# Writing a sparse gate matrix by indirect scatter transfers instead of one-hot matmuls, in a one-core PEER layer on Trainium2

## The chip, the cores and the metric

The kernel runs on one core of one Trainium2 chip. The time is the device time of one launch, in microseconds (us). Before the change it is 4085.16 us, the median of three runs (4085.02 to 4093.54).

## What is computed

One inference step of a one-layer encoder for 544 tokens (512 of a prompt, 32 of a sample), width 2048, in float32. First a convolution group and a gated linear attention group are mixed and normalised. Then comes the PEER mixer, in which the change lies:

```python
q = (xt @ w_query).reshape(tp, PEER_HEADS, 2, PEER_DKEY // 2)
s = jnp.einsum('thpc,hpnc->thpn', q, sub_keys)
sv, si = lax.top_k(s, PEER_TOPK)                       # 8 heads, 2 x 128 keys, top 16
cand = sv[:, :, 0, :, None] + sv[:, :, 1, None, :]
cid = si[:, :, 0, :, None] * PEER_NKEYS + si[:, :, 1, None, :]
best, pos = lax.top_k(cand.reshape(...), PEER_TOPK)    # 16 of 256 pairs
ids = jnp.take_along_axis(cid..., pos, axis=-1)        # expert numbers, 0 to 16383
gates = jax.nn.softmax(best, axis=-1)
h = gelu(einsum('td,thkd->thk', xb, u_table[ids]))
out = einsum('thk,thkd->td', gates * h, v_table[ids])
```

So each token has 128 pairs (expert, gate); an expert can be picked by more than one head of a token, and its gates then add.

## The kernel before, in words

Engines are programmed by hand and joined by semaphores. Activations lie feature-major (128 features on the partitions, tokens along the row). A product in float32 is made of three products of split halves: each 128x2048 weight tile is loaded by SyncE (SP) into one of two buffers `wraw`, ScalarE (ACT) copies it to the reduced-precision `wh` (line 837), and another engine subtracts, `wl = wraw - wh`; TensorE (PE) then runs `xh*wh`, `xl*wh` and `xh*wl` over 16 feature tiles and two halves of the tokens, 96 matmuls of 128x272 a tile (`job`, line 522). GpSimd (POOL) makes all splits `wl` up to the last tile of U (`lo`, line 460, semaphore `wlo`); VectorE (DVE) makes those of V (`v_lo_split`, line 1502, semaphore `v_lo`). SP loads the next tile of a buffer when the split of its last one is done.

The stages, in time: input products, convolution and attention (to about 780 us of the profiled execution); `w_out` (16 tiles) with the first normalisation; `w_q` (16 tiles) with the key scores; **the U stage**, 128 tiles of the expert table U, which gives h for all 16384 experts and all tokens; **the V stage**, 128 tiles of V, which multiplies W = gate * h with V.

Of the 544 tokens 416 are handled densely (`TD`): for them the gates stand in a full matrix G of 16384 experts x 416 tokens, which lies in DRAM (`g_dram`) like h (`h_dram`). The other 128 tokens take their rows of V and their h one by one with indirect gathers by POOL in the V stage (`h_gather` and `v_gather`, lines 486 to 496; 128 of each, 128 elements of 4 bytes or 128 rows of 8 KB in one).

How G is made before: DVE does the top-k of the eight heads (lines 1411 to 1430), ACT and DVE the softmax (line 1077, lines 1433 to 1440); DVE makes the indices of the sparse tokens (lines 1445 to 1451). After 16 tiles of U (`U_A` = 4 loops of four) PE waits for the picks, turns them with 12 transposes (line 761) and waits for ACT's copy of them (line 1080). In the next 52 tiles of U (`U_B` = 13 loops of four) two `g_group`s follow each tile: for four tokens each, DVE writes one-hot rows (`oneA` in three bf16 parts that hold the gate, line 1468, and `oneB`, line 1469), PE multiplies them (12 matmuls of 128x128, line 745) into a 128x128 slice of G of that token, ACT copies the slices to `gst` (line 1087) and stores 2 MB per 32 tokens in DRAM (line 1098). The last 60 tiles of U (`U_C`) have no such work.

In the V stage the experts are taken in 16 groups of eight tiles. SP loads the group's G (`gt`) and h (`hg`), 1664 KB each (`group_in`, line 413), in the same queue as the tiles of V. The first group's load waits until all of G is stored. DVE makes `wt = hg * gt` and its split for the next group (`make_w`, line 1482), adds PE's results (line 1500), adds the sparse tokens' rows (line 1519) and splits V (line 1506). At the turn from U to V, DVE, ACT and DVE again make the first W in a chain (lines 1532, 1111, 1527), and POOL splits the second tile of V beside it.

Of the kernel before, what the change touches and what calls it, by code (L numbers as in the profile page):

```python
# [30 lines left out]
P = 128  # L31
# [15 lines left out]
TT = 5  # L47
# [11 lines left out]
G_AHEAD = 2  # L59
# [62 lines left out]
def program(nc, xT, w_in, w_f, w_out, w_q, u_t, v_t, conv_state, conv_w, conv_vec, gla_state,  # L122
# [3 lines left out]
    with ctx:  # L126
# [5 lines left out]
        def sem(name):  # L132
# [89 lines left out]
        picksT = at("picksT", [P, 3, TD], F32, S0 + 7840)  # L222
        gate_p = [at(f"gate_p{a}", [P, TD], F32, S0 + 12832 + a * ROWD) for a in range(3)]

        assert 12832 + 3 * ROWD == 17824
# [8 lines left out]
        OH = 2 * 4 * P * 2  # L234
        gst = [at("gst0", [P, P, GC], F32, M0 + 4 * ROW), at("gst1", [P, P, GC], F32, M1 + 4 * OH)]
        part = at("part", [P, TD], BF16, M1 + 4 * OH + P * GC * 4)
        oneA = [at(f"oneA{a}", [P, 2, 4, P], BF16, M1 + a * OH) for a in range(3)]
        oneB = at("oneB", [P, 2, 4, P], BF16, M1 + 3 * OH)

# [8 lines left out]
        gt = at("gt", [P, NGC, EG, GC], F32, S0)  # L248
# [44 lines left out]
        q_out, s_mm, s_out, topk_s, gd_s, ge_s, picks_s, pt_mm, pt_out = (  # L293
            sem("q_out"), sem("key_scores"), sem("key_scores_out"), sem("head_picked"), sem("gate_diff"),
            sem("gate_exp"), sem("picks_ready"), sem("picks_turned"), sem("picks_turned_out"))
        oneh, g_mm, g_out = sem("one_hots"), sem("g_mm"), sem("g_out")
        g_st, h_st = [sem("g_stored0"), sem("g_stored1")], [sem("h_stored0"), sem("h_stored1")]
# [8 lines left out]
        ids_s, rows_in, v_lo, slot_s, y_sp_s, y_turn = (  # L306
            sem("slot_ids"), sem("v_rows_laid"), sem("v_lo_split"), sem("slot_added"),
            sem("slots_done"), sem("slots_turned"))
        sh_in = [sem(f"slot_h_in{b}") for b in range(SLOTS // HB)]
        sv_in = [sem(f"slot_v_in{b}") for b in range(3)]  # L310

# [5 lines left out]
        h_dense = h_flat[NKEY * P * SD:].rearrange("(n p u t) -> n p u t", p=P, u=2, t=TD)  # L317
# [7 lines left out]
        U_A, U_B = 4, NGC  # L325
        U_C = NKEY // 4 - U_A - U_B
# [33 lines left out]
        def _(sp):  # L360
# [41 lines left out]
            with sp.Fori(0, NG) as g:  # L402
                for m in range(EG):
                    sp.wait_ge(wlo, g * EG + (A_U + m - 1))
                    tile(us[bass.ds(g, 1), m].rearrange("o p k c -> (o p) k c"), m % 2)
                    for d in range(2):
                        load(v_dst[bass.ds(g, 1), m, d].rearrange("o j e c -> (o j) e c"),
                             v_src[bass.ds(g, 1), m, d].rearrange("o j e c -> (o j) e c"), rows_in)
            gsrc = g_dram.rearrange("c j (g e) t -> g j c (e t)", e=EG)
            hsrc = h_dense.rearrange("(g n) p u t -> g p n (u t)", n=EG // 2)  # L410
            vs = v_t.rearrange("(g n u) p k c -> g n u p k c", u=2, n=EG // 2)

            def group_in(g):
                for dst, src, q in ((gt[:].rearrange("p c e t -> p c (e t)"), gsrc, g_in),
                                    (hg[:].rearrange("p (n u) t -> p n (u t)", u=2), hsrc, h_in)):
                    a = src[g] if isinstance(g, int) else src[bass.ds(g, 1)].rearrange("o p n q -> (o p) n q")
                    load(dst, a, q)

            def v_first():
                for m in range(4):  # L420
                    sp.wait_ge(wlo, A_V + m - 1)
                    tile(vs[0, m // 2, m % 2], m % 2)

            def v_pairs(g, i0, i1):
                with sp.Fori(i0, i1) as i:
                    for u in range(2):
                        sp.wait_ge(v_lo, (g * EG + (u - 3)) + i * 2)
# [9 lines left out]
            v_first()  # L437
# [19 lines left out]
        def _(pool):  # L457
# [26 lines left out]
            lo_pairs(A_Q // 2 + 1, A_V // 2 + 1)  # L484
# [34 lines left out]
        def _(pe):  # L519
            mat = nc.tensor.matmul  # L520

            def job(u, n, ah, al, out, waits, first_k=None, ks=range(KT), begin=True, end=True):


                if begin:
                    pe.wait_ge(wlo, n + 1)
# [13 lines left out]
            pe.sem_inc(g_mm, G_AHEAD)  # L540
# [193 lines left out]
            def u_tile(n, u):  # L734

                job(u, n + A_U, xh, xl, zr(u), [(h_out, n + 1)])

            def g_group(q, v, bank):

                pe.wait_ge(oneh, q + 1)  # L740
                pe.wait_ge(g_out, q + 1)
                for t in range(4):
                    o_ps = ps[:, bank, t * P:(t + 1) * P]
                    for a in range(3):
                        ins = mat(o_ps, oneB[:, v, t], oneA[a][:, v, t], start=(a == 0), stop=(a == 2))  # L745
                ins.then_inc(g_mm, 1)

            pe.wait_ge(q_out, NQ)
            with pe.Fori(0, U_A) as i:
                for w in range(4):  # L750
                    u_tile(i * 4 + w, w % 2)


            pe.wait_ge(picks_s, 1)
            pe.wait_ge(s_out, NQ)
            for a in range(3):
                for tt, (t0, m) in enumerate(TOPK_TILES):
                    if tt == SPARSE:
                        continue
# [902 lines left out]
```

## Time and profile before

| what | us |
|---|---|
| median of three runs | 4085.16 |
| lowest, highest | 4085.02, 4093.54 |
| the profiled execution, its own time | 4094.46 |
| its span in the profile | 4092.7 |

The profile is of one execution with a hardware profiler. Its page gives the busy time of each engine, the span in 40 slices of 102.3 us, the chain of work that ended last, and the costliest groups of instructions. "L534" is line 534 of the kernel. PE is TensorE, PEld its weight loads, DVE VectorE, ACT ScalarE, POOL GpSimd, SP the queue of SyncE; a name with a q (SPq, ACTq) is an engine's sequencer, which issues transfers. "Idle before" is the time in which an engine stood still just ahead of an instruction, with what ended it.

### The profile page before, as it was taken

To read this page: it belongs to the slowest core of one execution; us is meant where nothing else is said; L and a number is where in the kernel's file an instruction comes from. 1 tells how busy PE (TensorE), PEld (TensorE's weight loads), DVE (VectorE), ACT (ScalarE), POOL (GpSimd) and SP (SyncE) were. 2 spreads that over 40 slices of the span, in tenths; PEclk is the share of its full clock that TensorE was granted. 3 is DMA by queue.
4 is the path that set the end of the run, shared out by engine and by line. 5 is a ranking of instruction groups with operands and counts; after the bars stand their busy time and mean duration, and the time that the engine had idled before them with its cause. 6 is when DMAs were issued, how large, how long until landed. Compare 5 with 4: busy or idle time off the path is not lost.

```text
span 4092.7 us, 70828 instructions
## 1 busy us (share of the span) xinstructions
PE 3908.7 (96%) x27864; PEld 3831.7 (94%) x27864; DVE 2617.1 (64%) x4474; ACT 1051.8 (26%) x914; POOL 1470.2 (36%) x497
## 2 busy tenths in 40 slices
PE   8999998796999999999999999999999999999996
PEld 7999998796999999999999999999999999999995
DVE  5776957656899299999972000001587787887867
ACT  3222322323222233333332222222222221222213
POOL 3232332344333333333334333434444344442311
PEclk9988988898999999999999999999999999999998
DMA  3221221221235656666666666665677778778752
GB/s 136 79 72 59 81 65 72 80 82 52 82 123 166 199 192 211 218 224 210 225 213 200 198 194 199 198 199 192 234 266 293 294 287 313 265 286 311 279 208 85
DMA packets 416196, 751.55 MB, mean 184 GB/s; under 512 B 19600, under 2 KB 343632, under 8 KB 355296
## 3 DMA queue, kind: packets, MB, share of 16 engines
q1 hardware_dynamic: 351936, 543.27, 39.4%
q0 software_dynamic: 22528, 134.30, 8.2%
q10 hardware_dynamic: 41632, 72.67, 5.0%
q8 instruction: 61, 1.00, 0.1%
q14 instruction: 39, 0.32, 0.0%
HBM read 677.60 MB, written 206.78 MB: 216 GB/s over the span
## 4 chain that ended last, share of the span: by engine, by line
PE 76%; DVE 14%; DMA 4%; issue 2%; ACT 2%; POOL 1%; SPq 1%; ACTq 0%; DVEq 0%; POOLq 0%
PE ps L534 52%; PE ps L778 19%; DMA wraw<-in_v_t 4%; DVE yb L1305 2%; PE ps L745 2%; DVE wl L1506 2%; PE ps L656 1%; PE ps L611 1%; PE ps L658 1%; ACT wh L837 1%; SPq L362 1%; DVE acc L1500 1%; DVE y_sp L1519 1%; DVE yfb L1314 0%; POOL wl L464 0%
## 5 line engine op out<-in xcount | busy, mean ns | idle before, releaser
L464 POOL TENSOR_TENSOR wl<-wraw,wh 128x2048 fp32r<-128x2048 f32 x202 | 961.0, 4758 | 1753.3 <-ACT wh L837 1753.3
L534 PE MATMUL ps<-xh,wh 128*128 128x272 f32 x5888 | 1241.3, 292 | 50.8 <-POOL xl L483 22.0
L534 PE MATMUL ps<-xh,wl 128*128 128x272 f32 x5888 | 1228.6, 290 | 0.0
L534 PE MATMUL ps<-xl,wh 128*128 128x272 f32 x5888 | 1225.2, 290 | 0.0
L534 PEld LDWEIGHTS ps<-xh,wh 128*128 128x128 f32 x5888 | 935.2, 191 | 63.9 <-issue 52.7
L534 PEld LDWEIGHTS ps<-xl,wh 128*128 128x128 f32 x5888 | 936.1, 191 | 0.0
L534 PEld LDWEIGHTS ps<-xh,wl 128*128 128x128 f32 x5888 | 930.5, 191 | 0.0
L837 ACT ACTIVATE wh<-wraw 128x2048 fp32r<-128x2048 f32 x328 | 628.5, 1916 | 1145.5 <-PE ps L778 732.8
L778 PE MATMUL ps<-Wh,wh 128*128 128x416 f32 x2048 | 721.9, 352 | 29.3 <-DVE wl L1506 21.2
L778 PE MATMUL ps<-Wh,wl 128*128 128x416 f32 x2048 | 724.8, 354 | 0.0
L778 PE MATMUL ps<-Wl,wh 128*128 128x416 f32 x2048 | 717.4, 350 | 0.0
L1468 DVE TENSOR_SCALAR oneA<-iota,picksT,gate_p 128x128 bf16<-128x128 f32 x1248 | 577.5, 516 | 62.5 <-PE ps L745 62.1
L489 POOL DMA_INDIRECT gath<-v_rows,s_ids x128 | 301.9, 2359 | 594.2 <-DVE y_sp L1519 556.4
L1532 DVE TENSOR_TENSOR wt<-hg,gt 128x416 f32<-128x416 f32 x8 | 4.6, 591 | 670.2 <-PE ps L534 670.0
L778 PEld LDWEIGHTS ps<-Wh,wh 128*128 128x128 f32 x2048 | 386.3, 189 | 36.6 <-issue 34.3
L778 PEld LDWEIGHTS ps<-Wl,wh 128*128 128x128 f32 x2048 | 386.7, 189 | 6.3
L778 PEld LDWEIGHTS ps<-Wh,wl 128*128 128x128 f32 x2048 | 385.9, 188 | 2.6
L1055 ACT ACTIVATE hb<-ps 128x544 f32<-128x544 f32 x128 | 79.9, 624 | 1144.5 <-PE ps L534 1144.5
L1506 DVE TENSOR_TENSOR wl<-wraw,wh 128x2048 fp32r<-128x2048 f32 x126 | 288.1, 2286 | 62.5 <-ACT wh L837 62.3
L1519 DVE SCALAR_TENSOR_TENSOR y_sp<-gath,s_w,y_sp 128x2048 f32<-128x2048 f32 x127 | 298.7, 2352 | 5.7
L1500 DVE TENSOR_TENSOR acc<-acc,ps 128x416 f32<-128x416 f32 x256 | 150.0, 586 | 183.7 <-PE ps L778 179.2
L1305 DVE SCALAR_TENSOR_TENSOR yb<-ext,cwt,yb 128x574 f32<-128x574 f32 x232 | 212.7, 978 | 1.7
(235 smaller groups left out, 2906.4 us busy)
## 6 DMA issues: line engine op xcount, KB each, us to landing
wraw<-in_u_t SPq DMA_DIRECT2D x128, 1024.0 KB, 5.0
v_rows<-in_v_t SPq DMA_DIRECT2D x256, 512.0 KB, 6.9
wraw<-in_v_t SPq DMA_DIRECT2D x128, 1024.0 KB, 5.1
wraw<-in_w_in SPq DMA_DIRECT2D x40, 1024.0 KB, 5.0
h_scratch<-hb ACTq DMA_DIRECT2D x64, 416.0 KB, 3.9
g_scratch<-gst ACTq DMA_DIRECT2D x13, 2048.0 KB, 7.7
gt<-g_scratch SPq DMA_DIRECT2D x16, 1664.0 KB, 14.1
hg<-h_scratch SPq DMA_DIRECT2D x16, 1664.0 KB, 20.5
```

Source lines behind the costliest of these rows:

```text
L464: nc.gpsimd.tensor_tensor(wl[:, u], wraw[:, u], f(wh[:, u]), ALU.subtract).then_inc(wlo, 1)
L489: nc.gpsimd.indirect_dma_start(gath[s % 3][:], None, v_rows, bass.IndirectOffsetOnAxis(ap=s_ids[:, s:s + 1], axis=0)).then_inc(sv_in[s % 3 ...
L534: ins = mat(out[:, h], w[:, u, k], m[:, k, halves[h]], start=(begin and k == ks[0] and w is wh and m is ah), stop=(end and k == ks[-1] and ...
L745: ins = mat(o_ps, oneB[:, v, t], oneA[a][:, v, t], start=(a == 0), stop=(a == 2))
L778: ins = mat(yd(u, d), w[:, u, d * EG + e], m[:, e], start=(e == 0 and w is wh and m is Wh[v]), stop=(e == EG - 1 and w is wl))
L837: go(wh[:, u], wraw[:, u], ACT.Copy).then_inc(whi, 1)
L1055: C.done(go(parts(hb[:, w // 2, w % 2]), zr(w % 2), ACT.Gelu), h_out)
L1305: ins = stt_(y_[:], rows, tap, y_[:], ALU.mult, ALU.add)
L1468: ts_(oneA[a][:, u, t], iota[:], picksT[:, 1, tok], gate_p[a][:, tok], ALU.is_equal, ALU.mult)
L1500: C.done(tt_(a_, a_, yd(n % 2, d), ALU.add), y_add)
L1506: C.inc(tt_(wl[:, n % 2], wraw[:, n % 2], f(wh[:, n % 2]), ALU.subtract), v_lo)
L1519: C.inc(stt_(y_sp[:], gath[s % 3][:], s_w[:, s:s + 1], y_sp[:], ALU.mult, ALU.add), slot_s)
```

## The change

G in DRAM is laid out anew, as (group, row of 128, expert tile in the group, token), and is cleared: ACT stores a block of zeros (128 x 4 x 416, 832 KB) 32 times during the `w_out` stage, two stores after each tile. DVE sets the block once ahead of that stage, and waits for the 32 stores before it writes the first `x2t`, since the block lies in that place. After the softmax DVE computes the element number of each pick in G, and POOL issues 512 indirect transfers (8 heads x 16 ranks x 4 tiles of tokens), each of which adds up to 128 elements of 4 bytes from SBUF to G in DRAM (`compute_op=add`); a token is one partition, so the elements of one transfer differ. Between two heads POOL waits until all transfers of the heads before have landed. SP waits for the last before it loads the first group.

The transposes, one-hots, G matmuls, G copies and 2 MB stores are gone. POOL splits tiles up to the 16th of U only; DVE splits from there on (`lo` on DVE, semaphore `dlo`, `D0` = 16 tiles after the start of U), the first two of V included, and computes `acc` between the first 16 of these splits. The h scratch is laid out so that a partition's part of a group is one run; the loads of `gt` and `hg` each read one run of 13,312 bytes per partition where they read 13 runs of 1 KB and 4 runs of 3,328 bytes.

```diff
+        g_col = [at(f"g_col{i}", [P, TT, P], dt, S0 + 7840 + i * TT * P * 4) for i, dt in enumerate((F32, F32, U32))]
+        g_idx = g_col.pop()
+        zeros = at("zeros", [P, 4, TD], F32, S0)
...
-        gt = at("gt", [P, NGC, EG, GC], F32, S0)
+        gt = at("gt", [P, EG, TD], F32, S0)
...
+        g_rows = g_flat.rearrange("(g j e t) -> g j e t", j=P, e=EG, t=TD)
...
+        h_dense = h_flat[NKEY * P * SD:].rearrange("(g p n u t) -> g n p u t", g=NG, p=P, u=2, t=TD)
...
+        D0 = A_U + 4 * U_A
...
@@ block.sync, loads of U @@
+            with sp.Fori(3, NG) as g:
+                for m in range(EG):
+                    sp.wait_ge(dlo, g * EG + (A_U + m - 1 - D0))
+                    u_tile_in(g, m)
...
-            for v in range(2):
-                sp.wait_ge(g_st[v], 16 * (NGC // 2 + 1))
+            sp.wait_ge(g_put, 16 * len(G_TILES) * SLOTS)
             for v in range(2):
                 sp.wait_ge(h_st[v], 32 * (EG // 4))
             group_in(0)
-            v_first()
+            v_pairs(0, 0, EG // 4)
...
@@ block.gpsimd @@
-            lo_pairs(A_Q // 2 + 1, A_V // 2 + 1)
+            lo_pairs(A_Q // 2 + 1, D0 // 2)
...
+            pool.wait_ge(g_ids, 1)
+            pool.wait_ge(g_zero, 16 * 2 * NG)
+            for h in range(PH):
+                if h:
+                    pool.wait_ge(g_put, 16 * len(G_TILES) * TOPK * h)
+                for k in range(TOPK):
+                    for tt in G_TILES:
+                        m, c = TOPK_TILES[tt][1], h * TOPK + k
+                        nc.gpsimd.indirect_dma_start(
+                            g_elem, bass.IndirectOffsetOnAxis(ap=g_idx[0:m, tt, c:c + 1], axis=0),
+                            picks[0:m, 0, tt, h, k:k + 1], None, compute_op=ALU.add).then_inc(g_put, 16)
...
@@ block.tensor, U stage @@
-            pe.wait_ge(picks_s, 1)
...
-                    ins = nc.tensor.transpose(ps[:, 4 + a, t0:t0 + m], src, ident[0:m, 0:m])
-            ins.then_inc(pt_mm, 1)
-            pe.wait_ge(pt_out, 1)
-            with pe.Fori(0, U_B) as i:
+            with pe.Fori(U_A, NKEY // 4) as i:
                 for w in range(4):
-                    u_tile(i * 4 + (4 * U_A + w), w % 2)
-                    for q in range(2):
-                        g_group(i * 8 + (2 * w + q), q, 4 + (2 * w + q) % 4)
...
+                    n = i * 4 + w
+                    job(w % 2, n + A_U, xh, xl, zr(w % 2), [(h_out, n + 1)], split=(dlo, n + (A_U + 1 - D0)))
...
@@ block.scalar, w_out stage @@
                     go(sq[:], r1[:, bass.ds(n, 1)].rearrange("p o t -> p (o t)"), ACT.Square).then_inc(rsq_s, 1)
+                    a.wait_ge(zero_set, 1)
+                    g = g_rows[bass.ds(n, 1)].rearrange("o j e t -> (o j) e t")
+                    for e in (0, 4):
+                        a.dma_start(g[:, e:e + 4], zeros[:]).then_inc(g_zero, 16)
...
@@ block.vector @@
+            nc.vector.memset(zeros[:], 0.0).then_inc(zero_set, 1)
             nc.vector.memset(sum1[:], 0.0)
...
             norm_stats(D, sum1, sum2, tmp[0], yr)
+            v_.wait_ge(g_zero, 16 * 2 * NG)
...
-            v_.wait_ge(pt_out, 1)
...
+            C.done(cp(g_idx[:], flat(1)), dve)
+            C.done(ts_(g_idx[:], g_idx[:], EG - 1, None, ALU.bitwise_and), dve)
+            C.done(cp(g_col[0][:], g_idx[:]), dve)
+            C.done(ts_(g_col[0][:], g_col[0][:], float(TD - P * TD), None, ALU.mult), dve)
+            C.done(stt_(g_col[1][:], flat(1), float(P * TD), g_col[0][:], ALU.mult, ALU.add), dve)
+            C.done(stt_(g_col[0][:], flat(2), float(EG * TD), g_col[1][:], ALU.mult, ALU.add), dve)
+            for tt in G_TILES:
+                ins = ts_(g_col[1][:, tt], g_col[0][:, tt], s_tok[:], float(TOPK_TILES[tt][0]), ALU.add, ALU.add)
+            C.done(ins, dve)
+            for tt in G_TILES:
+                ins = cp(g_idx[:, tt], g_col[1][:, tt])
+            C.done(ins, g_ids)
+
+            def lo(n, u):
+                v_.wait_ge(whi, n + 1)
+                v_.wait_ge(mm, n - 1)
+                C.inc(tt_(wl[:, u], wraw[:, u], f(wh[:, u]), ALU.subtract), dlo)
+
+            with C.loop(KT // 2, {dlo: 2, dve: 4}) as i:
                 for u in range(2):
-                    v_.wait_ge(g_mm, i * 2 + (u + 1))
...
+                    lo(i * 2 + (D0 + u), u)
+                    kk = bass.ds(i * 2 + u, 1)
+                    C.done(ts_(one(acc[:, kk]), one(f(xh[:, kk])), ALPHA, None, ALU.mult), dve)
+                    C.done(stt_(one(acc[:, kk]), one(f(xl[:, kk])), ALPHA, one(acc[:, kk]), ALU.mult, ALU.add), dve)
+            with C.loop((A_V + 2 - D0 - KT) // 2, {dlo: 2}) as i:
+                for u in range(2):
+                    lo(i * 2 + (D0 + KT + u), u)
             v_.sem_inc(acc_set, 1)
```

## Rows read from the trace of the kernel before

**Rows 1.** The page: the DMA engines' busy tenths in 40 slices

```profile
DMA  3221221221235656666666666665677778778752
```

**Rows 2.** The page: the chain that ended last, shares by engine

```profile
PE 76%; DVE 14%; DMA 4%; issue 2%; ACT 2%; POOL 1%; SPq 1%; ACTq 0%; DVEq 0%; POOLq 0%
```

**Rows 3.** The chain in time: start, us, engine, tile, line, count; U stage to V

```profile
1249.02 170.60 PE ps L534 x1344
1423.64 13.81 PE ps L534 x96
...
2123.91 721.66 PE ps L534 x5760
...
2853.42 156.30 PE ps L778 x816
```

**Rows 4.** Groups of instructions over the whole span

```profile
L464 POOL TENSOR_TENSOR wl<-wraw,wh 128x2048 fp32r<-128x2048 f32 x202 | 961.0, 4758 | 1753.3 <-ACT wh L837 1753.3
...
L1506 DVE TENSOR_TENSOR wl<-wraw,wh 128x2048 fp32r<-128x2048 f32 x126 | 288.1, 2286 | 62.5 <-ACT wh L837 62.3
...
L745 PE MATMUL ps<-oneA,oneB 128*128 128x128 bf16 x1248 | 78.7, 219 | 0.0
```

**Rows 5.** What PE waited for: first 1225 to 2850, then 2840 to 4060 us

```profile
PE ps L534 <- ACT picksT L1080: 2.2, 1, 2.2
...
PE ps L778 <- DVE wl L1506: 21.2, 13, 5.7
PE ps L778 <- DVE Wl L1527: 7.9, 1, 7.9
```

**Rows 6.** Timeline of ACT before the 17th tile of U (start, us)

```profile
1384.21 1.92 ACT L837 ACTIVATE wh<-wraw 128x2048 fp32r<-128x2048 f32 x1
...
1396.24 1.92 ACT L837 ACTIVATE wh<-wraw 128x2048 fp32r<-128x2048 f32 x1
```

**Rows 7.** Timeline of DVE, softmax and the indices of the sparse tokens

```profile
1376.35 0.82 DVE L1438 TENSOR_REDUCE gsum<-picks 128x40 f32<-128x640 f32 x1 [32.48 <-ACT picks L1077]
...
1377.64 1.92 DVE L1440 TENSOR_TENSOR picks<-picks,gsum 128x640 f32<-128x640 f32 x1
...
1381.16 0.23 DVE L1451 CAST s_hid<-s_h 128x128 uint32<-128x128 f32 x1
```

**Rows 8.** Timeline of POOL, the first 32 gathers of h, back to back

```profile
2852.99 1.28 POOL L494 DMA_INDIRECT s_h<-h_scratch,s_hid  x1 [0.16 <-issue]
...
2866.92 2.88 POOL L494 DMA_INDIRECT s_h<-h_scratch,s_hid  x1 [0.31 <-issue]
...
2901.32 0.94 POOL L489 DMA_INDIRECT gath<-v_rows,s_ids  x1 [0.30 <-issue]
```

**Rows 9.** Timeline of DVE beside the second row above

```profile
2866.68 2.29 DVE L1506 TENSOR_TENSOR wl<-wraw,wh 128x2048 fp32r<-128x2048 f32 x1 [1.29 <-ACT wh L837]
```

**Rows 10.** The gathers of V rows (ns, min/median/max), and landing of the h gathers

```profile
L489 POOL DMA_INDIRECT gath<-v_rows,s_ids x128: 937/2748/3008, 2901.3 to 3940.3; - x128
...
DMA to landing us min/median/max: 4.4/6.7/10.9
```

**Rows 11.** Windows: w_out, then U alone (PE, PEld, DVE, ACT, POOL busy, PEclk, DMA, GB/s)

```profile
780.00:950.00 170.00, 170.00 (x1336) 170.00 (x1337) 97.38 (x57) 32.68 (x27) 66.72 (x14) 0.98 0.25 86
...
2200.00:2400.00 200.00, 200.00 (x1599) 200.00 (x1598) 0.00 (x0) 40.65 (x32) 77.03 (x17) 1.00 0.61 196
```

**Rows 12.** DMA issues on SP: KB each, median us to landing

```profile
gt<-g_scratch SPq DMA_DIRECT2D x16, 1664.0 KB, 14.1
hg<-h_scratch SPq DMA_DIRECT2D x16, 1664.0 KB, 20.5
```

**Rows 13.** Timeline of SP: first group's load, and one in the V stage

```profile
2807.39 2.46 SPq L362 DMA_DIRECT2D gt<-g_scratch  x1
...
3679.06 9.79 SPq L362 DMA_DIRECT2D hg<-h_scratch  x1
```

**Rows 14.** Timeline of DVE, the first write of x2t

```profile
970.05 1.36 DVE L1385 TENSOR_TENSOR x2t<-r,sum 128x544 f32<-128x544 f32 x2 [0.79 <-ACT sum L854]
```

More of the change, by code:

```diff
@@ L401, in _, with u_tile_in @@
             v_dst = v_rows.rearrange("(g e j) (i d c) -> g i d j e c", e=EG, j=P, i=EG, d=2)
-            with sp.Fori(0, NG) as g:
+            def u_tile_in(g, m):
+                a = us[g, m] if isinstance(g, int) else us[bass.ds(g, 1), m].rearrange("o p k c -> (o p) k c")
+                tile(a, m % 2)
+                for d in range(2):
+                    to = v_dst[g, m, d] if isinstance(g, int) else v_dst[bass.ds(g, 1), m, d].rearrange("o j e c -> (o j) e c")
+                    fr = v_src[g, m, d] if isinstance(g, int) else v_src[bass.ds(g, 1), m, d].rearrange("o j e c -> (o j) e c")
+                    load(to, fr, rows_in)
@@ L403, in _ @@
+            with sp.Fori(0, 2) as g:
                 for m in range(EG):
                     sp.wait_ge(wlo, g * EG + (A_U + m - 1))
[L405 to L409, printed above, removed]
@@ L410, in _ @@
-            hsrc = h_dense.rearrange("(g n) p u t -> g p n (u t)", n=EG // 2)
+                    u_tile_in(g, m)
+            assert D0 == A_U + 2 * EG
+            for m in range(EG):
+                if m < 2:
+                    sp.wait_ge(wlo, D0 + m - 1)
+                else:
+                    sp.wait_ge(dlo, m - 1)
+                u_tile_in(2, m)
+            with sp.Fori(3, NG) as g:
+                for m in range(EG):
+                    sp.wait_ge(dlo, g * EG + (A_U + m - 1 - D0))
+                    u_tile_in(g, m)
@@ L411, in _ @@
+            gsrc = g_rows.rearrange("g j e t -> g j (e t)")
             vs = v_t.rearrange("(g n u) p k c -> g n u p k c", u=2, n=EG // 2)
             def group_in(g):
[L414 to L422, printed above, removed]
+                for dst, src, q in ((gt, gsrc, g_in), (hg, h_group, h_in)):
+                    a = src[g] if isinstance(g, int) else src[bass.ds(g, 1)].rearrange("o p q -> (o p) q")
+                    load(dst[:].rearrange("p e t -> p (e t)"), a, q)
             def v_pairs(g, i0, i1):
@@ L520, in _, with job @@
             mat = nc.tensor.matmul
-            def job(u, n, ah, al, out, waits, first_k=None, ks=range(KT), begin=True, end=True):
+            def job(u, n, ah, al, out, waits, first_k=None, ks=range(KT), begin=True, end=True, split=None):
                 if begin:
-                    pe.wait_ge(wlo, n + 1)
+                    s, v = split or (wlo, n + 1)
+                    pe.wait_ge(s, v)
                     for s, v in waits:
@@ L1101, in _ @@
[L1101 to L1107 removed]
+            u_four(1, 1)
+            with C.loop(NG - 2, {h_out: EG}) as g:
+                for i in range(2):
+                    u_four(g + 2, i)
             for e in range(EG):
@@ L1137, in _ @@
             a.wait_ge(cst_out, 32)
-            for v in range(2):
-                a.wait_ge(g_st[v], 16 * (NGC // 2 + 1))
+            a.wait_ge(g_zero, 16 * 2 * NG)
             for v in range(2):
@@ L1473, in _, with flat @@
-            v_.wait_ge(g_mm, TD // 4 + G_AHEAD)
-            for v in range(2):
-                v_.wait_ge(g_st[v], 16 * (NGC // 2 + 1))
-            with C.loop(KT, {dve: 2}) as k:
-                kk = bass.ds(k, 1)
-                C.done(ts_(one(acc[:, kk]), one(f(xh[:, kk])), ALPHA, None, ALU.mult), dve)
-                C.done(stt_(one(acc[:, kk]), one(f(xl[:, kk])), ALPHA, one(acc[:, kk]), ALU.mult, ALU.add), dve)
+            def flat(a):
+                return picks[:, a].rearrange("p t h k -> p t (h k)")
```

140 lines of the change are left out of this document (36 added, 104 removed).

## The prediction, made before the changed kernel ran

> **What bounds the kernel now.** I read the page's chain first: 76% of it is PE [rows 2]. Then the same chain in order of time. In the U stage it is PE tile after tile; from the 17th tile, which starts at 1423.64 us, to 2123.91 us lie the 52 tiles with G work, then 60 tiles without take 721.66 us, and at 2853.42 us V starts [rows 3]. PE's waits in the U stage are one: 2.2 us for ACT's copy of the turned picks [rows 5]. So between 1249 and 2845 us the time is the length of PE's own list, and whatever leaves that list leaves the time, as long as no other engine or transfer comes later than PE. In the V stage PE waits 21.2 us for DVE's V splits in 13 places and 7.9 us once for the first W [rows 5]; the DMA engines are busier there (tenths of 7 and 8) than in the U stage (6) [rows 1].
>
> **The change, part by part.**
>
> 1. *G work leaves PE.* With it a tile takes (2123.91 - 1423.64)/52 = 13.47 us, without it 721.66/60 = 12.03 us [rows 3]. Gain 52 x 1.44 = 74.8 us. (The 1248 matmuls are listed with 78.7 us busy [rows 4], the same size.)
>
> 2. *Transposes and the wait for their copy.* The 16th tile ends at 1249.02 + 170.60 = 1419.62, the 17th starts at 1423.64 [rows 3]: gain 4.0 us. DVE's one-hots and ACT's copies were beside PE and give nothing.
>
> 3. *Does DVE split in time?* The 17th tile's `wh` is copied at 1396.24 to 1398.16 [rows 6]; the DVE split takes 2.29 us where POOL's takes 4.76 [rows 4], so `wl` can stand at 1400.5, 19 us before PE wants it at 1419.6. Ahead of it on DVE stands the new index work. It begins after 1381.16 + 0.23 = 1381.4 [rows 7]: six instructions over 640 columns and eight over 128. A pass over 640 columns took 0.82 us and one took 1.92 [rows 7]; with 0.3 for each small one the whole is 7.3 to 13.9 us, done at 1388.7 to 1395.3, before the split. Cost nothing; its cover is 19 us. Later each tile gives DVE 2.3 us (4.3 with `acc`) in 12.03. The next load of a buffer is issued when the split is done, so it starts 2.5 us earlier than now. No gain from that, as PE never waited for `wl` here [rows 5].
>
> 4. *POOL's 512 scatters.* POOL's last split, of tile 16, starts when ACT ends at 1386.13 [rows 6] and takes 4.76: POOL is free at 1390.9. Take 1391 as the first scatter, 1395 at the latest. No scatter stands in the trace. Nearest are the gathers of h, also 128 elements of 4 bytes: the first 32, back to back, took from 2852.99 to 2901.32 [rows 8], 1.51 us apart. A quiet one takes 0.94, and one took 2.88, having started in the 0.24 us behind a DVE split of 2.29 us, which it outlasts [rows 8, 9]; in the U stage DVE splits once in 12.03 us, less often than there, so 1.51 is a fair pitch. The far end is the V-row gather, median 2.75 [rows 10] and 0.3 of issue: 3.05. I take 1.51, because size and count of the elements agree: 512 x 1.51 = 773 us, and seven waits between heads of 6.7 us each, the landing of an h gather [rows 10], 47 us. G is complete at 1391 + 820 = 2211 us. It is wanted when SP comes to the first group's load: that is at 2807.39 now [rows 13], 38 us before the U stage ends at 2845.57; after the change U ends at 1419.62 + 112 x 12.03 = 2767, so at 2729. Slack 518 us; cost nothing. The cover is gone at a pitch of (2729 - 1391 - 47)/512 = 2.52 us.
>
>    The Trainium skill ("SBUF — State Buffer", section "Summary: rules for kernel authors") says that GpSimd and a DVE instruction with two SBUF inputs block one another fully when GpSimd reads SBUF too, and that descriptor generation starves under DVE's faster modes. The 2.88 us row agrees with blocking. If every scatter met a whole split, the pitch would be near the V-row gather's, which is the far end above.
>
> 5. *What the DMA engines carry.* The U stage alone has them at 0.61 [rows 11]. 416 tokens x 128 picks over 16 engines are 3328 elements each. In the 1338 us from 1391 to 2729 the free share is 0.39 x 1338 = 522 us, or 0.157 us per element. The h gathers fed 8 elements per engine every 1.51 us (0.19 each) into a V stage of 7 tenths [rows 1] that hardly stopped PE [rows 5]; the price of an element that is read, added and written in DRAM isn't shown. Below it may be hidden, above 0.157 it may stretch the U stage; I take hidden, the nearest row being the gather.
>
> 6. *The clearing.* 32 stores of 832 KB in a stage that moves 86 GB/s at a share of 0.25 [rows 11]; two per tile of about 12 us add 142 GB/s, 228 in all, no more than the V stage moves. ACT is busy 32.68 of 170 us there [rows 11] and takes two issues in. The last pair is issued near 955; if it takes 14.1 us, as the twice as large load of `gt` [rows 12], it lands at 969, and DVE wants it at 970.05 [rows 14]. Cost 0, bounds 0 and 10 (it may share the engines with the first loads of `w_q` and the keys). The memset runs beside PE's first tile.
>
> 7. *The turn to V.* PE waits 7.9 us now [rows 5], since DVE's first split of W is held up by POOL's split of the second V tile. In its place DVE makes that split first: Gelu and ACT's copy of 1.92 us [rows 6], DVE's split 2.29 [rows 4], then product, copy and split of one 128x416 slice; with an estimated 0.6 us for each of the four short ones it is 6.6 us, with handovers 7. Gain 1, bounds -3 and 4.
>
> 8. *The V stage.* `gt` and `hg` come in long runs. Their loads take 14.1 and 20.5 us to land [rows 12], and one issue held SP for 9.79 us [rows 13], with the V tiles' loads behind it in the queue. If shorter runs were the reason, both shrink, and the waits for V splits go with them: 21.2 us is the most, 0 the least. I take 12.
>
> Sum: 74.8 + 4.0 + 1 + 12 = 91.8 us. The profiled execution took 4094.46 us, which becomes 4002.7. It stands 9.3 us over the median of the runs, 4085.16, so for the median 4085.2 - 91.8 = 3993 us. Without the 12 us it is 4005, with all 21.2 it is 3984.
>
> **Rivals.**
>
> *A. The issue of scatters is slow (slower than before).* Place: SP's wait for the last scatter. Each scatter costs 3.05 us, as the V-row gathers. Then G is complete at 1391 + 512 x 3.05 + 47 = 3000 us. The first group wants 38 us more to V's start, as now: 3038 against 2774 in my forecast, so 264 us late, 3993 + 264 = 4257 us. It turns to slower from a pitch of 2.52 + 91.8/512 = 2.70 us. For it: the accumulate form may need more per element than a gather, and those V-row gathers stood beside DVE's work. Against: the V-row gathers come singly, right as a DVE split starts; back to back the same form took 0.94 [rows 8].
>
> *B. The elements are taken one after another (slower by far).* An h gather's 8 elements per engine land in 6.7 us [rows 10], 0.84 us each. Gathers overlap, 4 of them in flight at a pitch of 1.51. If an add in DRAM does not overlap, because a read must come back before its write, then 3328 x 0.84 = 2787 us, G is complete at 4178, and the end is near 3993 + (4178 + 38 - 2774) = 5435 us. In milder form, 0.5 us per element, 1664 us, it is 3993 + 319 = 4312 us. The Trainium skill ("DMA: Bandwidth & Descriptors", section "Rules for kernel authors") says that the accumulate reads its destination and writes it later, with nothing held in between. Its section "Anatomy of one DMA — SWDGE (gpsimd) path" gives about 2.0 us fixed for one transfer; 512 of them one behind another would be an estimated 1024 us and still be hidden.
>
> *C. Issue hidden, loads late.* The elements cost 0.2 us of the DMA engines each: 666 us against 522 free, the U stage is stretched by up to 144 us for tiles that wait for their load: 3993 + 144 = 4137 us at the worst; a half of that, 4065, is still faster. Against: a buffer's load is issued some 5 us after a tile ends (copy 1.92 us [rows 6], split 2.29 [rows 4] and Gelu) and is wanted 24.06 us after it, so it may take 19 us.
>
> *D. The V loads do not get shorter and the clearing is late:* 4005 + 10 = 4015 us, still faster. It is a part of the forecast's own range, 3980 to 4020.
>
> **How the numbers follow.** Forecast with D: 0.64. C: 0.06, half on either side of before. A, and pitches between 2.52 and 3.05: 0.14, of which 0.02 end below the time before. B: 0.16. A measurement of this kernel can tell about 0.2%, 8 us, from no change. Faster: 0.64 + 0.02 + 0.02 = 0.68; same 0.02; slower 0.30. The range must leave out no more than 0.2: from 3980 over D, C and A to 4260 it leaves out B and little else. The likeliest case's own range is 3980 to 4020.
>
> **What the profile of the changed kernel would show.** Right: tiles of U 12.03 us apart from 1249 us to about 2767; no wait of PE for `wl` there; 512 DMA_INDIRECT on POOL from 1391 us, about 1.5 apart in runs of 64, ending near 2211; DMA share in that time under 0.9; V starting at about 2774; PE's waits in V under 21 us. Wrong: SP idle until POOL's last scatter lands, with PE waiting in front of V (A, B; a POOL that is busy means A, a POOL that waits between heads or stands in long issues means B); tiles of U further apart with PE waiting for ACT's and DVE's splits (C); DVE's first `x2t` later than 970 (D).

## The result, and the profile after

The changed kernel takes 3978.55 us in the median of four runs (3974.40 to 3983.18), the kernel before 4089.32 in its four; the ratio is 0.9729, 95% interval 0.9715 to 0.9743. The forecast was 3993 us with a range from 3980 to 4260. The direction and the likeliest case were right, and the time lies 1.5 us under the range. The profiled execution took 3983.18 us, 111.3 less than the one before.

From the page of the kernel after, its span, two engines and the DMA slices:

```profile
span 3981.4 us, 64674 instructions
...
PE 3814.9 (96%) x26604; PEld 3745.5 (94%) x26604; DVE 2230.6 (56%) x2933; ACT 939.1 (24%) x809; POOL 1821.2 (46%) x895
...
DMA  3211222353225677777777777665578778777752
```

The chain that ended last in the kernel after, in order of time (start, us):

```profile
770.58 171.01 PE ps L554 x1344
...
1239.28 1517.51 PE ps L554 x12096
...
2763.74 809.71 PE ps L767 x4272
```

The U stage, broken up by the G work in [rows 3], is now one unbroken run of PE from its third tile on, 126 tiles from 1239.28 to 2756.79 us. That makes 12.04 us a tile.

Where the 111.3 us of the two profiled executions lie, with the starts of `w_out`'s run of tiles and the ends of U as the marks:

| stretch | before | after | gain |
|---|---|---|---|
| start to `w_out` | 779.96 | 770.58 | 9.4 |
| `w_out` to the end of U | 2065.6 | 1986.2 | 79.4 |
| end of U to the first V matmul | 7.9 | 7.0 | 0.9 |
| V and the rest | 1239.3 | 1217.7 | 21.6 |

The first row is a stretch that the change does not touch. The last is larger than the 12 us of the forecast.

The scatters, DVE's U splits and PE's V matmuls in the list of groups of the kernel after:

```profile
L513 POOL DMA_INDIRECT g_scratch<-picks,g_col x512 | 869.9, 1699 | 199.5 <-issue 179.5 <-DMA g_scratch<-picks,g_col 19.9
...
L1437 DVE TENSOR_TENSOR wl<-wraw,wh 128x2048 fp32r<-128x2048 f32 x114 | 261.5, 2294 | 1099.8 <-ACT wh L824 1005.6
```

All seven waits between heads together are 19.9 us. What PE waited for from 2760 to 3960 us, which answers to [rows 5]:

```profile
PE ps L767 <- DVE Wl L1494: 7.0, 1, 7.0
PE ps L767 <- DVE wl L1473: 4.5, 3, 2.5
```

POOL's timeline of the first scatters and of the last, and below it DVE's split and index work beside them:

```profile
1393.21 1.72 POOL L513 DMA_INDIRECT g_scratch<-picks,g_col  x1 [0.17 <-issue]
...
1398.97 1.35 POOL L513 DMA_INDIRECT g_scratch<-picks,g_col  x1 [0.30 <-issue]
1400.62 3.59 POOL L513 DMA_INDIRECT g_scratch<-picks,g_col  x1 [0.30 <-issue]
1404.52 1.55 POOL L513 DMA_INDIRECT g_scratch<-picks,g_col  x1 [0.30 <-issue]
...
2459.97 2.47 POOL L513 DMA_INDIRECT g_scratch<-picks,g_col  x1 [0.30 <-issue]
```

```profile
1371.52 0.49 DVE L1421 CAST g_col<-picks 128x640 uint32<-128x640 f32 x1
...
1376.27 5.04 DVE L1431 CAST g_col<-g_col 128x128 uint32<-128x128 f32 x4
1400.50 2.29 DVE L1437 TENSOR_TENSOR wl<-wraw,wh 128x2048 fp32r<-128x2048 f32 x1 [19.19 <-ACT wh L824]
```

From 1393.21 to 2459.97 lie 511 steps: 2.09 us each with the waits between heads, 2.05 without them, where the forecast had 1.51 without them. A quiet scatter takes 1.55 us (1.35 with the 32-token tile) and 0.30 of issue. The one that starts at 1400.62 runs into DVE's split of 1400.50 to 1402.79 and takes 3.59, which is 2.04 more. The split had 2.17 us left when that scatter started. The Trainium skill ("SBUF — State Buffer", section "Summary: rules for kernel authors") has a GpSimd operation that reads SBUF and a DVE instruction with two SBUF inputs block each other fully; these rows agree. Besides, POOL stops for 1.7 to 5.7 us after every 72nd scatter, seven times and 26 us more than the usual 0.30 in all; the profile puts these stops to issue, and what they are is not shown. The four small casts at the end of the index work took 5.04 us together, beside POOL's own split (1376.48 to 1381.08); the index work ended at 1381.3, well before DVE's first U split at 1400.50.

The clearing cost nothing. The first `x2t` is written 189.9 us after the start of `w_out`'s run (190.1 before, [rows 14]); the stores land in 5.0 us each:

```profile
960.44 1.36 DVE L1349 TENSOR_TENSOR x2t<-r,sum 128x544 f32<-128x544 f32 x2 [0.78 <-ACT sum L839]
```

```profile
g_scratch<-zeros ACTq DMA_DIRECT2D x32, 832.0 KB, 5.0
```

### The profile page after: what moved, and what is told of

Read it like the earlier page. It is cut to its first block, busy times and chain, and to the rows that moved or that the text cites. A ratio compares the mean times of both kernels' runs of the same rounds, so it can differ in the third digit from the quotient of the medians.

```text
span 3981.4 us, 64674 instructions
## 1 busy us (share of the span) xinstructions
PE 3814.9 (96%) x26604; PEld 3745.5 (94%) x26604; DVE 2230.6 (56%) x2933; ACT 939.1 (24%) x809; POOL 1821.2 (46%) x895
## 4 chain that ended last, share of the span: by engine, by line
PE 82%; DVE 13%; DMA 1%; ACT 1%; issue 1%; POOL 1%; SPq 0%; DVEq 0%; ACTq 0%; POOLq 0%
PE ps L554 51%; PE ps L767 27%; DVE yb L1267 2%; DMA wraw<-in_v_t 1%; PE ps L675 1%; PE ps L677 1%; PE ps L630 1%; DVE dist L1155 1%; DVE qe L1186 1%; POOL wl L471 0%; PE ps L660 0%; DVE sif L1379 0%; ACT wh L824 0%; DVE si L1365 0%; DVE oh L1392 0%
## 5 line engine op out<-in xcount | busy, mean ns | idle before, releaser
L513 POOL DMA_INDIRECT g_scratch<-picks,g_col x512 | 869.9, 1699 | 199.5 <-issue 179.5
L1437 DVE TENSOR_TENSOR wl<-wraw,wh 128x2048 fp32r<-128x2048 f32 x114 | 261.5, 2294 | 1099.8 <-ACT wh L824 1005.6
L471 POOL TENSOR_TENSOR wl<-wraw,wh 128x2048 fp32r<-128x2048 f32 x88 | 429.3, 4880 | 824.9 <-ACT wh L824 824.9
L496 POOL DMA_INDIRECT gath<-v_rows,s_ids x128 | 313.3, 2448 | 560.5 <-DVE y_sp L1486 522.1
L501 POOL DMA_INDIRECT s_h<-h_scratch,s_hid x128 | 156.6, 1223 | 339.6 <-issue 339.6
L1473 DVE TENSOR_TENSOR wl<-wraw,wh 128x2048 fp32r<-128x2048 f32 x126 | 288.0, 2286 | 23.6 <-ACT wh L824 21.9
```

Of the source, the lines that this page charges most:

```text
L471: nc.gpsimd.tensor_tensor(wl[:, u], wraw[:, u], f(wh[:, u]), ALU.subtract).then_inc(wlo, 1)
L496: nc.gpsimd.indirect_dma_start(gath[s % 3][:], None, v_rows, bass.IndirectOffsetOnAxis(ap=s_ids[:, s:s + 1], axis=0)).then_inc(sv_in[s % 3 ...
L501: nc.gpsimd.indirect_dma_start(s_h[:, s:s + 1], None, h_elem, bass.IndirectOffsetOnAxis(ap=s_hid[:, s:s + 1], axis=0)).then_inc(sh_in[s // ...
L513: nc.gpsimd.indirect_dma_start(g_elem, bass.IndirectOffsetOnAxis(ap=g_idx[0:m, tt, c:c + 1], axis=0), picks[0:m, 0, tt, h, k:k + 1], None, ...
L1437: C.inc(tt_(wl[:, u], wraw[:, u], f(wh[:, u]), ALU.subtract), dlo)
L1473: C.inc(tt_(wl[:, n % 2], wraw[:, n % 2], f(wh[:, n % 2]), ALU.subtract), dlo)
```

## The experiments

All are edits of the kernel after unless said otherwise. "V stretch" is the time from the end of U to the end of the span: 1247.1 us before, 1224.6 after.

### Both kernels again: where the first 9.4 us come from

> The kernel before, profiled a second time. Theory: of the 111.3 us between the two profiled executions 9.4 us lie before the w_out stage, which the change does not touch, and are a difference between executions; then this profile either starts w_out's run of tiles near 770 us instead of 779.96, or shows 780 again while the repeated profile of the kernel after moves. Rival: something of the change (the semaphores set at the start, the place of the code) makes the first stage shorter; then this one starts near 780 and the kernel after near 770, both times.

> The kernel after, profiled a second time. If the first stage differs from execution to execution, its w_out run of tiles starts somewhere between 768 and 781 us; if the change shortens it, at 770.6 within 1 us. In both theories U takes 1517.5 us, the last scatter is issued near 2460 us and the V stage takes 1176 us from its first matmul to the last mean.

No edit. The kernel before took 4085.15 us, the kernel after 3990.13. A third execution of the kernel after stands further down. The marks of the five:

| execution | `w_out` starts | from there to the end of U | V stretch |
|---|---|---|---|
| before | 779.96 | 2065.6 | 1247.1 |
| before, again | 773.94 | 2064.8 | 1244.6 |
| after | 770.58 | 1986.2 | 1224.6 |
| after, again | 781.54 | 1983.3 | 1223.5 |
| after, third | 779.16 | 1983.3 | 1224.2 |

The start of `w_out` moves by 6 us between the two executions of the kernel before and by 11 us between the three of the kernel after, and their ranges overlap. So the 9.4 us need no effect of the change; the expectation had one of the two kernels move, and both did. Two windows of equal place in the kernel after, first and second execution, show what differs with it (columns as in [rows 11]):

```profile
260.00:390.00 130.00, 124.97 (x926) 117.31 (x926) 91.05 (x115) 41.68 (x48) 33.77 (x7) 0.93 0.19 65
...
260.00:390.00 130.00, 126.30 (x918) 119.11 (x917) 95.04 (x117) 39.16 (x44) 34.01 (x7) 0.90 0.20 72
```

The granted clock is 0.93 in the one and 0.90 in the other. What makes the clock differ is not shown. The other two stretches repeat within 3 us. Those of the U stage lie in its run of 126 tiles, which came out at one of two lengths, 1517.51 us in the first execution after and 1514.23 in the second; why is not shown. The change itself is worth 2065.2 - 1984.3 = 81 us up to the end of U and 1245.9 - 1224.1 = 22 us behind it, 103 in all. Of the 110.8 us between the first medians some 8 belong to the draw of executions (which of them happened to be measured); against further runs of the kernel before, the repeated kernel after had a ratio of 0.9757 (0.9732 to 0.9783).

### The layouts of before: what the V stage gained from

```diff
-        h_dense = h_flat[...].rearrange("(g p n u t) -> g n p u t", ...)
+        h_dense = h_flat[...].rearrange("(g n p u t) -> g n p u t", ...)
...
-            gsrc = g_rows.rearrange("g j e t -> g j (e t)")
+            gsrc = g_dram.rearrange("c j (g e) t -> g j c (e t)", e=EG)
...
+            C.done(ts_(g_col[0][:], flat(1), float(GC), None, ALU.mult), dve)
+            C.done(stt_(g_col[1][:], flat(2), float(P * GC), g_col[0][:], ALU.mult, ALU.add), dve)
```

> The kernel after with the two DRAM layouts of before: G as 13 runs of 1 KB and h as 4 runs of 3328 bytes per partition and group. The scatters go to other addresses, 512 of them as before. Theory (the V stage gained because the group loads got shorter): PE's waits for V splits come back, about 21 us instead of 4.5, the clock dips behind them come back, and the V stage is some 17 to 21 us longer: profiled 4000 to 4004 us, ratio to before 0.977 to 0.978. Rival (the V stage gained from something else, such as the order of loads after the first group): it stays within 3 us of 3983.

Measured: 4003.29 us (4001.87 to 4004.85), ratio 0.9801 (0.9781 to 0.9821). The theory's gain and place are right, the time is in its range, the ratio a little above it. V stretches by windows, of the kernels before and after and of this one:

```profile
2845.60:4092.00 1246.40, 1175.96 (x6168) 1157.99 (x6168) 957.55 (x955) 272.94 (x170) 478.53 (x267) 0.98 0.69 258
```

```profile
2756.80:3981.00 1224.20, 1171.27 (x6168) 1157.49 (x6168) 955.19 (x956) 273.20 (x170) 486.80 (x266) 0.98 0.68 263
```

```profile
2753.00:4001.00 1248.00, 1179.02 (x6168) 1160.30 (x6168) 955.55 (x956) 273.10 (x170) 476.32 (x266) 0.98 0.69 258
```

The stretch is 23.7 us longer than in the kernel after. PE is busy 7.8 us longer for the same 6168 matmuls (first pair of numbers), and its waits for V splits are 16.0 us longer (20.5 against 4.5). Between before and after the same sum is 4.7 + 16.7 = 21.4 of the 21.6 us. So the waits cost more than themselves. A part of that is the clock: behind three of the fifteen waits here, of 2.1 to 3.4 us, the granted clock falls to 0.50 for some 3 to 7 us, as in the second of these windows; behind the others it stays at 1.00, as in the first.

```profile
3315.00:3320.00 5.00, 4.14 (x23) 3.76 (x22) 4.49 (x7) 2.29 (x2) 0.00 (x0) 1.00 0.74 259
...
3841.00:3845.00 4.00, 3.04 (x9) 2.91 (x10) 3.86 (x8) 1.91 (x1) 0.00 (x0) 0.50 0.48 145
```

The kernel before has such a fall behind two of its thirteen waits (2.1 and 5.7 us), the kernel after behind one of three (2.5 us). The length of the wait alone does not decide it: one of 3.0 us in the kernel before left the clock at 1.00.

Each layout by itself:

> The kernel after with G alone in the layout of before (13 runs of 1 KB per partition and group); h stays one run. The run with both short took 1248.3 us from the end of U to the end of the span where the kernel after took 1224.6, with PE waits for V splits of 20.5 us against 4.5. Theory (number of runs decides: 1664 of the 2176 pieces of a group are G's): most of it is G's, 1240 to 1247 us and waits of 12 to 20 us. Rival (it is h's, whose issue held SP for 9.8 us before): 1224 to 1230 us, waits under 8.

> The kernel after with h alone in the layout of before (4 runs of 3328 bytes). Theory: little, 1225 to 1232 us from the end of U to the end of the span, PE waits for V splits under 9 us. Rival (h's share): 1240 or more.

Edits: of the diff above only the G lines, or only the h lines. Measured: G alone 3992.76 us (ratio 0.9784, 0.9767 to 0.9802), h alone 3986.80 (0.9762, 0.9745 to 0.9780). The V stretches are 1227.8 and 1227.6, each some 3 us longer than after. PE's waits and the median landing of the `hg` load, for both, G alone and h alone:

```profile
PE ps L770 <- DVE wl L1478: 20.5, 15, 3.4
...
hg<-h_scratch SPq DMA_DIRECT2D x16, 1664.0 KB, 20.9
```

```profile
PE ps L770 <- DVE wl L1478: 7.8, 5, 2.9
...
hg<-h_scratch SPq DMA_DIRECT2D x16, 1664.0 KB, 18.3
```

```profile
PE ps L769 <- DVE wl L1475: 6.1, 3, 3.1
...
hg<-h_scratch SPq DMA_DIRECT2D x16, 1664.0 KB, 17.0
```

The theory that G's 13 runs carry it failed (1240 to 1247 us were expected with G alone), and so did the reading that h does; "little" was right for h alone. Either long run is enough. The landing times suggest why: with 17.0 or 18.3 us for `hg` the V tile queued behind it is still in time, with 20.9 it is not (20.5 before, [rows 12]; the page of the kernel after gives none, other executions with both runs long have 15.6). The chains that ended last agree: V tiles' loads have 3.8% of the span before and 4.7% with both layouts short, but 1.2% with G alone, 1.0% with h alone and 0.9% after. No run sets the landing time by itself, so this step stays argued. SP's long issue of `hg` is not the cause: it is there with G alone too, at no great cost. The instructions of SP for both loads, with both short and with G alone:

```profile
L363 SPq DMA_DIRECT2D hg<-h_scratch x16: 877/4612/9938, 2715.1 to 3811.8; - x16
```

```profile
L363 SPq DMA_DIRECT2D hg<-h_scratch x16: 875/4510/9882, 2728.5 to 3803.9; - x16
```

### A scatter that only writes: what the add costs

```diff
-                            picks[0:m, 0, tt, h, k:k + 1], None, compute_op=ALU.add).then_inc(g_put, 16)
+                            picks[0:m, 0, tt, h, k:k + 1], None).then_inc(g_put, 16)
```

> The kernel after with the scatters as plain writes, without the add: where two heads of a token pick the same expert the later gate stands alone. Theory (the cost of a scatter on POOL is that of making its descriptors, and the add makes it dearer than the gather's 0.94 us): the quiet scatter falls from 1.55 us to about 0.95 to 1.3, the last one is issued near 2150 to 2300 us instead of 2460, the DMA share in that time falls from 0.76 to 0.66 to 0.70, and the time stays at 3983 within 8 us, as all of it is hidden. Rival (a scatter is dearer because it writes DRAM by indices, add or not): 1.55 us and a share of 0.76 stay.

Measured: 3986.07 us; scatters of 0.96 us in the median from 1400.7 to 2160.9, 1.49 apart. Windows of the U stage: the kernel after with scatters and behind them, and this one with scatters.

```profile
1450.00:2440.00 990.00, 990.00 (x7905) 990.00 (x7904) 202.08 (x107) 208.31 (x164) 807.12 (x476) 1.00 0.76 197
2480.00:2700.00 220.00, 220.00 (x1759) 220.00 (x1758) 41.82 (x19) 48.27 (x38) 0.00 (x0) 1.00 0.62 196
```

```profile
1450.00:2150.00 700.00, 700.00 (x5590) 700.00 (x5589) 146.44 (x82) 147.34 (x116) 534.28 (x469) 1.00 0.64 198
```

The theory holds; the DMA share, 0.64, fell a little below the 0.66 to 0.70 expected. The plain scatter is the h gather of [rows 8] in price and nearly in pace (1.49, with the waits between heads, against 1.51). The add makes it 0.6 us longer on POOL, and takes 0.14 of the DMA engines' time where the plain write takes 0.02. With 6.5 elements per scatter and engine in the mean that is 0.14 x 2.09 / 6.5 = 0.045 us per added element. PE is busy all of the time in all three windows.

### Four heads scattered twice: how much cover is left

```diff
-            for h in range(PH):
-                if h:
-                    pool.wait_ge(g_put, 16 * len(G_TILES) * TOPK * h)
+            for q, h in enumerate(list(range(PH)) + [0, 1, 2, 3]):
+                if q:
+                    pool.wait_ge(g_put, 16 * len(G_TILES) * TOPK * q)
...
+            C.done(ts_(picks[:, 0, :, 0:4], picks[:, 0, :, 0:4], 0.5, None, ALU.mult), dve)
```

> The kernel after with 256 more scatters: the gates of four heads are halved and added twice, so G is the same. Theory (the scatters are free until SP wants the first group near 2716 us and then cost one for one): at 2.08 us each and some 5 us per head the last one is issued near 3000 us; V starts some 20 us behind, near 3020 instead of 2764; span near 3981 + 255 = 4236 us. PE stands still in front of V for about 260 us. Rival (part of the issue time is pressure from the U stage's splits and loads, which ends with U): the scatters issued after 2757 us come at 1.85 us, and V starts near 2990.

Measured: 4219.87 us, span 4218.0. POOL's last scatter, SP's load of the first group, PE's first V matmul, and a window in which POOL works alone:

```profile
2980.30 1.34 POOL L513 DMA_INDIRECT g_scratch<-picks,g_col  x1 [0.30 <-issue]
```

```profile
2982.91 0.35 SPq L362 DMA_DIRECT2D gt<-g_scratch  x1
```

```profile
3005.39 0.69 PE L767 MATMUL ps<-Wh,wh 128*128 128x416 f32 x1 [237.05 <-DVE Wl L1496]
```

```profile
2780.00:2980.00 200.00, 0.00 (x0) 0.00 (x0) 0.00 (x0) 0.00 (x0) 164.01 (x110) 0.50 0.21 0
```

SP's load follows the last scatter within 2.6 us, and V starts 22.5 us behind that. This execution began `w_out` 11.1 us later than the profiled kernel after, so V starts 3005.39 - 2763.74 - 11.13 = 230.5 us late. The theory's wait for the last scatter is right; in size the rival (V near 2990, plus the 11 us) is nearer than its 3020 plus 11. The 110 scatters of the lone window come 1.82 us apart, as no DVE split blocks POOL there. This is the place and the mechanism of rival A of the prediction, reached by more scatters instead of dearer ones: slower than before by PE standing in front of V. The kernel after has 2716 - 2460 = 256 us of cover.

### POOL splits again, beside the scatters

```diff
+            for n in range(D0, A_V):
+                lo(n, n % 2, n - 1)
+                for h, k, tt in todo[:5]:
+                    ...
+                    nc.gpsimd.indirect_dma_start(g_elem, ..., compute_op=ALU.add).then_inc(g_put, 16)
+                todo = todo[5:]
...
-                    job(..., split=(dlo, n + (A_U + 1 - D0)))
+                    job(...)
```

> The kernel after with the U splits given back to POOL, five scatters behind each split; DVE splits from the first V tile. Theory (moving the splits is a needed part of the change, as POOL has no room for both): POOL needs 4.8 + 5 x 1.85 = 14.0 us per tile where PE needs 12.03, so 102 tiles take 14.0 to 14.5 us each and the span grows by 200 to 250 us, to about 4200, slower than before. Rival (the splits could have stayed; the scatters are cheap once DVE does not block POOL, or POOL's split hides in the transfer's own time): tiles stay at 12.03 us and the span within 10 us of 3981.

Measured: 4187.81 us, span 4186.0, 205 us over the kernel after and 108 over the median of the runs of the kernel before beside it (4079.98). PE's waits between 1225 and 2750 us, and a window of the U stage:

```profile
PE ps L554 <- POOL wl L471: 9.6, 1, 9.6
...
PE ps L557 <- POOL wl L471: 152.0, 82, 9.6
...
1800.00:2600.00 800.00, 712.97 (x5506) 701.89 (x5505) 0.00 (x0) 147.03 (x116) 695.65 (x344) 0.98 0.65 170
```

The first line is the kernel after, the other two this one. U goes on to some 2961 us here, so the 152.0 are not all of its waits. A tile takes 13.95 us in the window (5506 matmuls in 800 us, 96 to a tile), just under the 14.0 to 14.5 expected, and the span grew by 204.6 us. The theory holds: handing the splits to DVE is a needed half of the change. With it POOL's 1067 us of scatters lie beside PE; without it they come in front of each tile.

### Two reorderings that the traces point to

The turn to V (7.0 us of waiting) and the first normalisation, where POOL and DVE block each other:

```diff
@@ turn @@
+                if not (isinstance(n, int) and n == NKEY - 1):
+                    hi(n + (A_U + 2), w % 2, None)
...
                 go(Wh[0][:, e], wt[e % 2][:], ACT.Copy).then_inc(wh_s, 1)
+                if e == 1:
+                    hi(A_V + 1, 1, None)
...
+                if e == 5:
+                    lo(A_V + 1, 1)
@@ normalisation, the second kernel only @@
-                nc.gpsimd.tensor_tensor(xl[:, k], x2t[k % 4][:], f(xh[:, k]), ALU.subtract).then_inc(x2_s, 1)
...
+                C.inc(tt_(xl[:, k], x2t[k % 4][:], f(xh[:, k]), ALU.subtract), x2_s)
```

> The kernel after with the turn from U to V reordered: ACT makes the first two slices of Wh before it copies the second V tile, and DVE splits that tile after the sixth product of W instead of ahead of the first. Theory (PE waits 7.0 us there for a Gelu, a copy and a V split that it does not need first): PE's wait falls to some 2 us, with up to 1 us given back when it reaches the later slices; V starts 4 to 5 us earlier against the end of U. Rival (the low clock behind the wait or the later V split takes it back): the stretch from the end of U to the end of the span stays at 1224 us within 1.5.

> The same, and besides the 16 splits of the first normalisation made by DVE instead of POOL, so that the two no longer block each other (DVE's subtraction takes 0.71 us alone and 1.85 to 3.64 beside POOL's split). Theory: a pair of feature tiles takes 4.2 us of DVE where the two engines together take 5.37, so PE's 22 us of waits in front of w_q fall by 6 to 9 us; with the turn the time is 10 to 14 us under the kernel after, ratio to before near 0.970. Rival (PE itself, at the lower clock, is the pace there): the stretch from the first x2t to the first whole w_q tile stays as long, and only the turn's 4 to 5 us come.

> The kernel after, timed on the same chip beside the run above: ratio to before 0.973 within 0.002, and 8 to 14 us above the run with both reorderings. If the two intervals overlap wholly, the reorderings are not worth measuring in the total.

Measured: the turn alone 3984.63 us in one execution; both reorderings 3971.06 (3966.01 to 3976.24), ratio 0.9719 (0.9694 to 0.9744); the kernel after 3988.44 (3980.14 to 3991.71), ratio 0.9757 (0.9732 to 0.9783). PE's waits, first in the turn alone, then in front of `w_q` with both reorderings, then there in the kernel after:

```profile
PE ps L767 <- DVE Wl L1500: 3.0, 1, 3.0
```

```profile
PE ps L551 <- DVE xl L1349: 16.4, 5, 13.1
```

```profile
PE ps L554 <- POOL xl L490: 22.0, 7, 13.7
```

The turn's wait falls by 4.0 us, to 3.0 where 2 were expected, and the V stretch to 1220.7, 3.9 under the first execution after: the theory's lower end. In the normalisation the waits fall by 5.6 us, just under the 6 to 9 expected; the first whole tile of `w_q` starts at 1010.86 - 777.56 = 233.3 us after the start of `w_out`, where the kernel after has 1022.51 - 779.16 = 243.4. DVE's subtraction of the mean takes 1.36 us for two features throughout; beside POOL every other one took 1.85 for a single feature. Of these 10 us some 7 are left at the end of U (1976.4 against 1983.3 from the start of `w_out`). The other 3 lie in the run of U's tiles, here first in the kernel after, third execution, then with both reorderings:

```profile
1248.21 1514.21 PE ps L554 x12096
```

```profile
1236.46 1517.53 PE ps L551 x12096
```

These are the two lengths that the kernel after itself shows, so they need not come from the reordering. The five runs of the one lie all under the five of the other. The medians are 17.4 us apart, more than the 10 to 14 and the 8 to 14 expected, and the kernel after came out at 0.9757 where 0.971 to 0.975 was expected; the stretches behind the start of `w_out` account for 10.8 us in the two profiled executions. The ratio intervals, which carry the spread of the kernel before, touch at 0.973 to 0.974.

## Why the prediction was right or wrong

**Step 1 and 2, G work and transposes: right.** 78.8 us forecast; 79.4 in the first pair and 81 over five executions, of which the length of U's run of tiles (1517.51 or 1514.23 us) makes up to 3. The prediction's "PE's waits in the U stage are one: 2.2 us" left one out: the same view has 9.6 us for POOL's split in front of the third tile. It is there in both kernels, so the sum did not suffer.

**Step 3, DVE splits in time: right.** PE waits for one split in U, the 9.6 us in front of the third tile, as before. The index work took 9.8 us (7.3 to 13.9 forecast), with half of it the casts beside POOL's split.

**Step 4, POOL's scatters: the mechanism right, the term mis-sized.** "I take 1.51, because size and count of the elements agree" held for a plain scatter (1.49) and not for one that adds (2.05, and 2.09 with the waits between heads). Those waits were 19.9 us and not 47. G was complete near 2465 us and not 2211. The cover of 518 us swallowed it and 256 are left; above a pitch of 2.52 it would not have. The range from 1.51 to 3.05 held the value, and the choice of its lower end rested on the shape of the transfer alone, without the add.

**Step 5, the DMA engines: right.** 0.76 of their time with the scatters. An added element costs 0.045 us where 0.157 was free.

**Step 6 and 7, clearing and turn: right.** 0 and 0.9 us.

**Step 8, the V stage: the step that failed, by its size.** "21.2 us is the most, 0 the least. I take 12." Measured 21.6. The direction (long runs, loads that land earlier) was right, and the layouts of before bring it all back. Two things were wrong in it. The bound counted PE's waits alone, but PE was also busy 4.7 us less for the same matmuls, in part because the granted clock falls behind some of the waits; so 21.2 was not the most. And the middle was taken between bounds where 16.7 of the 21.2 us went, with either of the two layouts alone giving most of it. With 21.6 in the place of 12 the forecast is 3983.4 us: this step is 9.6 of the 14.5 us between forecast and measurement, but alone it would not have left the range.

**The draw: a term put at nothing.** The sum was made on one execution and moved by 9.3 us to the median. The range's low end, 3980, left 4 us below "with all 21.2 it is 3984" for everything else, and the spread of the first stage (11 us between executions of one kernel) was in no bound. With 103 us for the change and a before of 4085.16 the forecast would have been 3982, still inside the range; the four runs gave 3978.55, and the five of the later comparison 3988.44. That the time lies 1.5 us below the range and not inside it is thus in part luck of the draw. A low end at 3970 was due.

**The rivals.** A and B did not happen; the doubled heads show that A's place and mechanism are real, with 256 us to spare. B's one-after-another is refuted by scatters 2.09 us apart with waits of 19.9 us in all between heads. The Trainium skill's fixed 2.0 us per transfer ("DMA: Bandwidth & Descriptors", section "Anatomy of one DMA — SWDGE (gpsimd) path") is near the 2.09 by chance: the plain form came 1.49 us apart, below it, since transfers overlap. C did not happen. D's late clearing did not either.

## What to carry to other kernels

Work that fills a busy engine in order to place few values can go to scattering transfers, if the engine that issues them is first freed of what stands in front of the bound, and if the clearing and the wait for the last transfer have cover; count the issue time by the form that is really used, adding or plain. When waits of TensorE are removed, look at the granted clock behind them as well: the fall behind a few of them goes with them. And before a range is narrowed to tens of microseconds in four thousand, look at how much the untouched stages move from one execution to the next.

## What the runs showed of the hardware

- An indirect transfer of 128 elements costs POOL 0.94 us as a gather, 0.96 as a scatter, 1.55 as a scatter that adds; with 32 elements the last is 1.34 to 1.35. Most of it does not depend on the number of elements.
- Adding 4-byte elements in DRAM takes a DMA engine about 0.05 us each: 0.14 of its time beside the U stage, and 0.21 in the window without other transfers (0.21 x 1.82 / 6.5 = 0.059).
- Giving all two-input work to DVE can be faster than sharing it with POOL: 16 splits moved from POOL to DVE, and a pair of features went from 5.4 to 4.1 us.
- Scatters that add, issued back to back, pause after every 72nd: seven times among 512, for 1.7 to 5.7 us, and at the same steps among the 768 of the doubled heads, for up to 6.4. The plain scatters paused only between heads. The cause is not shown.
- Behind a wait of 2.1 to 5.7 us for a V split the granted clock of TensorE fell to 0.50 in six cases, for some 3 to 7 us; behind others of 2.3 and 3.0 us it stayed at 1.00.
